# Four neighbouring rows of a down-projection chunk in one partition, with gate and up columns read with a step of four

## The chip, the cores and the metric

The kernel runs on one core of one Trainium2 chip. The metric is the device time of one execution in microseconds (us), the median of several executions. The engines are TensorE (PE; its loads of the stationary operand are shown as PEld), VectorE (DVE), ScalarE (ACT), GpSimd (POOL) and SyncE (SP), which issues nearly all DMAs; 16 DMA engines move the data.

## What is computed

Two layers of an encoder for 256 rows (tokens) of 1024 features in float32. Each layer has a mixer (three kinds of attention between two projections) and a mixture of experts. The change touches only the experts. Cut to them, the reference is:

```python
# per token: one of 4 groups, then 2 of its 8 experts; 32 experts per layer
def expert_block(args):
    xb, e = args
    h = jax.nn.silu(xb @ w_gate[e]) * (xb @ w_up[e])   # (rows, 1024) @ (1024, 512), twice
    return h @ w_down[e]                               # (rows, 512) @ (512, 1024)
```

The result of each token's two experts is multiplied by its gates and added to x. The weights w_gate and w_up are (2, 32, 1024, 512) and w_down is (2, 32, 512, 1024), all float32, so each expert has three matrices of 2 MiB.

## The kernel before

**Weights.** A ring of eight slots of 16 KB per partition (`ring`, lines 181 and 46 to 47) takes every large weight as a chunk of 2 MiB, one DMA each, issued by SP in a fixed order (lines 366 to 393): six chunks of the input projection, two of the output projection, and then per expert gate, up and down. A chunk goes into slot c % 8. Before each issue SP waits for the slot's semaphore `slot_free` (line 389); PE raises it when it is through with the chunk (lines 1419, 1420 and 1441). Each slot has a semaphore `slot_full` that the DMA raises on landing and that PE waits for (line 1397). Since the eight slots are in use one after the other, the DMAs run ahead of PE by up to eight chunks. All experts are computed for every layer, whichever tokens chose them, for at most 32 tokens each; a loop for experts with more tokens follows (line 1462) and does nothing with these inputs.

**Layouts.** The views at lines 309 and 310 put rows 8p to 8p+7 of gate and up into partition p, which are 8 x 512 neighbouring numbers of the tensor, 16 KB. The view at line 311 puts rows p, 128+p, 256+p and 384+p of down into partition p, four pieces of 1024 numbers (4 KB). The chunk views at lines 313 to 318 only name the 4096 numbers of a partition as (8, 512) or (4, 1024).

**The work per expert on PE** (lines 1444 to 1455; `ROUNDS` is 4 rounds of `BODY` = 8 experts, each with two groups of four). `tokens` gathers the tokens of four experts at once into `xg` by matmuls with a 0/1 matrix (line 1353). `products` waits for gate and up and runs `gate_up` (line 1364): for each of the eight row blocks j, four matmuls of 32 stationary columns (the tokens) and 256 moving columns (weights). The four go to four column groups of the array (tile_position 0, 32, 64, 96): gate's first and second half, up's first and second half. They write 4 x 32 partitions of `gu_ps`. The trace has two matmul records for each float32 matmul, so 64 per expert. ACT copies `gu_ps` to `h_rows` (line 616, recorded at its helper's line 466). `turned` releases the gate and up slots and transposes `h_rows` in two blocks of 128 columns (line 1372), after which partition d of block c holds column 128c + d of each half; it also transposes the gates (line 1374). ACT and DVE form silu(gate) x up in `hid` (lines 595, 963 to 971). `down` (line 1380) runs, for k = 0 to 3, a matmul of `hid[:, b, k % 2, k // 2]` with `down_chunk(s)[:, k]`: block k % 2 and half k // 2 of `hid` must be the expert features that row k of the down chunk holds in each partition. ACT copies the result to `y`, and `scatter` (line 1388) multiplies it by the transposed gates and adds it into four banks for all 256 tokens.

The order in the steady state is written out by hand: products(e), down_of(e-1), turned(e), add(e-1). PE is in order, so a wait for a chunk in `products` holds all behind it.

Other lines that the prediction speaks of: line 680 and line 877 (DVE, the normalised rows; both write with a step of 128 numbers, except line 680 in its last use), line 871 (DVE, an addition of 512 contiguous numbers), line 1333 (PE, bf16 matmuls of zeros that keep it busy while the router's result is awaited), and line 369 (the chunks of the input projection, whose pieces are 512 numbers of a row, 2 KB).

Of the kernel before, what the change touches and what calls it, by code (L numbers as in the profile page):

```python
# [44 lines left out]
KE = D_EXPERT // P  # L45
SLOTS = 8
SLOT = KD * 512
CAP = 32
QUAD = P // CAP
HALF = D_EXPERT // 2  # L50
# [105 lines left out]
def trunk(nc, x_d, w_in, w_out, norm_mix, norm_ffn, rel_bias, lam_q1, lam_k1, lam_q2, lam_k2,  # L156
# [4 lines left out]
    with ctx:  # L161
# [13 lines left out]
        gu_ps = pv[:, 0, 0:HALF]  # L175
# [38 lines left out]
        def take(n):  # L214
            taken[0] += n
            assert taken[0] <= arena.shape[1]
            return arena[:, taken[0] - n:taken[0]]
# [24 lines left out]
        xg = take(2 * KD * P).rearrange("p (b j s) -> p b j s", b=2, j=KD)  # L242
# [65 lines left out]
        wout_v = w_out.rearrange("l (k p) n -> l p k n", k=KD)  # L308
        gate_v = w_gate.rearrange("l e (p j) d -> (l e) p j d", j=KD)
        up_v = w_up.rearrange("l e (p j) d -> (l e) p j d", j=KD)  # L310
        down_v = w_down.rearrange("l e (k p) n -> (l e) p k n", k=KE)

        def chunk(s, n):

            return ring[:, s, 0:KD * n].rearrange("p (j n) -> p j n", j=KD)
# [4 lines left out]
        def nk(t):  # L320
            return P * (t + 1)
# [735 lines left out]
        def _(pe):  # L1057

            mm, turn_ = nc.tensor.matmul, nc.tensor.transpose
# [8 lines left out]
            with pe.Fori(0, DEPTH) as l:  # L1068
# [34 lines left out]
                def z_rows(out, i, n, c, m, t):  # L1103

                    for j in range(KD):
                        ins = mm(out, xT[:, j, t * P:(t + 1) * P], chunk(i, n)[:, j, c:c + m],  # L1106
                                 start=(j == 0), stop=(j == KD - 1))
                    return ins
# [83 lines left out]
                for t in range(TOK):  # L1192
                    ins = z_rows(bank[:, 256 * t:256 * t + 256], 1, 512, 0, 256, t)
# [3 lines left out]
                for t in range(TOK):  # L1197
                    pe.wait_ge(cn_ready, at(l, 2, t + 1))
                    bank = tr_bank()
                    for k in range(3):  # L1200
                        ins = turn_(bank[:, k * P:(k + 1) * P], cn[:, t, k * P:(k + 1) * P], ident)
# [5 lines left out]
                for t in range(TOK):  # L1207
                    for k in range(2):
                        ins = mm(pv[:, 0, 192 * t:192 * t + 192], cT[:, k, t * P:(t + 1) * P], wuq[:, k, :],
                                 start=(k == 0), stop=(k == 1))  # L1210
# [8 lines left out]
                for u in range(0, 8, 2):  # L1219
                    t = u // 4  # L1220
                    banks = tr_bank(), tr_bank()
                    for m in range(2):
                        for i in range(2):
                            a = IDX_DIM * (u % 4 + i)
                            ins = mm(banks[i][:, m * nk(t):(m + 1) * nk(t)], zT[a:a + 32, 12 + m, t * P:(t + 1) * P],
                                     zT[a:a + 32, 14, 0:nk(t)], start=True, stop=True, tile_position=(a, 0))
# [5 lines left out]
                for pad in (qpad, kpad):  # L1232
                    bank = tr_bank()
                    for g in range(2):
                        for t in range(TOK):
                            ins = turn_(bank[:, g * SEQ + t * P:g * SEQ + (t + 1) * P],
                                        pad[:, t, 2 * g:2 * g + 2, :].rearrange("p h d -> p (h d)"), ident)
# [120 lines left out]

                def gate_up(sg, su, q, c):

                    halves = [chunk(s, 512)[:, :, h:h + HALF] for s in (sg, su) for h in (0, HALF)]
                    for j in range(KD):
                        for i, w in enumerate(halves):
                            ins = mm(gu_ps[i * CAP:(i + 1) * CAP, :], xg[:, q, j, c:c + CAP], w[:, j, :],  # L1364
                                     start=(j == 0), stop=(j == KD - 1), tile_position=(0, i * CAP),
                                     skip_group_check=True)
                    return ins
# [24 lines left out]
                with pe.Fori(0, ROUNDS) as m:  # L1392
# [13 lines left out]
                    def products(e):  # L1406

                        q, i, c = e // QUAD, e % QUAD, 3 * e
                        if i == 0:
                            pe.wait_ge(wide_read, at(r, WIDE, gather_use(q) + 1))  # L1410
                        landed(c)
                        landed(c + 1)
                        gate_up(c % SLOTS, (c + 1) % SLOTS, q, i * CAP).then_inc(gu_done, 1)
# [48 lines left out]
                with pe.If(more > 0):  # L1462
                    with pe.Fori(0, more) as k:
                        i = done + k
                        pe.wait_ge(o_pick, i + 1)
                        gather(0, CAP)[1].then_inc(o_wide, 1)
                        pe.wait_ge(o_wide_read, i * 2 + 1)
                        pe.wait_ge(over_full[0], i * 16 + 16)
                        pe.wait_ge(over_full[1], i * 16 + 16)
                        gate_up(0, 1, 0, 0).then_inc(o_gu, 1)  # L1470
                        pe.wait_ge(o_gu_read, i + 1)
                        turns(0, 0).then_inc(o_h, 1)
                        pe.wait_ge(o_hid, i + 1)
                        pe.wait_ge(over_full[2], i * 16 + 16)
                        down(2, 0, 0)
                        down(2, 0, 1).then_inc(o_wide, 1)
                        pe.wait_ge(o_wide, i * 2 + 2)
                        pe.sem_inc(over_free, 1)
                        pe.wait_ge(o_wide_read, i * 2 + 2)
                        pe.wait_ge(o_pgt_read, i + 1)  # L1480
                        scatter(0, 0)
                        scatter(0, 1).then_inc(o_comb, 1)
                pe.nop()

                for t in range(TOK):
                    for half in range(2):
                        ins = mm(acc[t][half], zeros[:, 0:P], zeros[:, P:P + 512], start=False, stop=True,
                                 skip_group_check=True)
# [43 lines left out]
```

## Time and profile before

| | us |
|---|---|
| Median of 3 runs | 1404.72 (1402.9 to 1407.91) |
| Profiled execution, its own time | 1402.78 |
| Its span, first to last instruction | 1400.2 |
| PE busy | 1109.2 (79%) |
| PE weight loads busy | 626.7 (45%) |
| DVE busy | 346.1 (25%) |
| ACT busy | 236.6 (17%) |
| POOL busy | 19.6 (1%) |

The span is the time between the first and the last instruction on the engines; the time of the execution has 2.6 us more around it. Busy shares are means over stages of different kinds: in each layer the mixer runs first, with few loads, and then the expert rounds, with loads all the time. PE's clock is given as the granted share of 2.4 GHz, and its mean over the span is 0.887. A time that a DMA takes "to landing" runs from its issue on SP's queue until its data have all arrived, so it contains the time in which the chunks ahead of it are moved.

### The profile page before, as it was taken

Reading aid. Unit: us, or ns where it says so; the run is one execution under the profiler, and the core shown is the slowest. Engines: PE = TensorE matmul, PEld = TensorE weight load, DVE = VectorE, ACT = ScalarE, POOL = GpSimd, SP = SyncE. Lnnn points to the kernel's source line nnn. Section 1 sums busy time; section 2 is a strip of 40 time slices with the busy share of each in tenths; the row PEclk is TensorE's granted clock in tenths of the full one; section 3 lists DMA queues with packets and bytes.
Section 4 is the critical chain, followed back from the end, with each engine's and each line's share of the span. In section 5 each row is a group of like instructions: output and inputs, shape, how many; then the busy total and the mean of one; then the engine's idle time right before and its main releaser. Section 6 shows DMA issues by size and latency. Waiting matters only on the chain.

```text
span 1400.2 us, 19949 instructions
## 1 busy us (share of the span) xinstructions
PE 1109.2 (79%) x7926; PEld 626.7 (45%) x7930; DVE 346.1 (25%) x954; ACT 236.6 (17%) x578; POOL 19.6 (1%) x45
## 2 busy tenths in 40 slices
PE   7379888888796877878779887898778777778776
PEld 3357645443443433344337664454344334434432
DVE  2035445312111211211121363551121121112112
ACT  2013321111111111111121242111111111111111
POOL 1000000000000000000000000000000000000000
PEclk9779889998898989899889888999799889889988
DMA  7592314799999999999995113069999999999993
GB/s 236 98 396 95 121 61 155 287 420 419 420 424 416 421 422 419 421 422 418 416 378 198 61 61 121 9 257 419 423 418 419 422 421 419 420 423 417 421 423 144
DMA packets 80143, 446.72 MB, mean 319 GB/s; under 512 B 9864, under 2 KB 15272, under 8 KB 63656
## 3 DMA queue, kind: packets, MB, share of 16 engines
q1 hardware_dynamic: 75816, 442.73, 78.3%
q10 hardware_dynamic: 4224, 2.46, 0.6%
q8 instruction: 84, 1.38, 0.4%
q14 instruction: 19, 0.16, 0.0%
HBM read 442.55 MB, written 2.62 MB: 318 GB/s over the span
## 4 chain that ended last, share of the span: by engine, by line
PE 49%; DMA 35%; issue 9%; DVE 3%; ACT 3%; ACTq 1%; POOL 0%; DVEq 0%; PEldq 0%; SPq 0%; POOLq 0%
DMA ring<-in_w_up 34%; PE pv L1364 14%; PE pj L1100 7%; PE tr L1380 5%; PE pj L1281 4%; PE pj L1106 3%; PE tr L1353 3%; PE pj L1388 3%; PE lg L1388 2%; ACT arena L466 2%; PE lg L1135 1%; PE pv L1166 1%; ACTq L350 1%; PE tr L1148 1%; PE pv L1301 1%
## 5 line engine op out<-in xcount | busy, mean ns | idle before, releaser
L1364 PE MATMUL pv<-ring,arena 128*32 128x256 f32 x4096 | 307.3, 464 | 162.6 <-DMA ring<-in_w_up 147.3
L1364 PEld LDWEIGHTS pv<-ring,arena 128*32 128x32 f32 x4096 | 165.3, 133 | 311.1 <-issue 211.7
L966 DVE TENSOR_SCALAR arena<-arena 128x128 f32<-128x128 f32 x64 | 14.5, 227 | 739.9 <-ACT arena L596 739.9
L466 ACT ACTIVATE arena<-tr 128x512 f32<-128x512 f32 (+3 forms) x200 | 111.2, 564 | 279.3 <-PE tr L1353 129.5
L1388 PE MATMUL pj<-arena 128*128 128x512 f32 x256 | 131.7, 596 | 0.0
L1388 PE MATMUL lg<-arena 128*128 128x512 f32 x256 | 130.7, 592 | 0.0
L466 ACT ACTIVATE arena<-pv 128x256 f32<-128x256 f32 x64 | 24.5, 383 | 581.7 <-PE pv L1364 581.7
L1380 PE MATMUL tr<-ring,arena 128*32 128x512 f32 x1024 | 122.1, 593 | 0.0
L1100 PE MATMUL pj<-xT,ring 128*128 128x256 f32 (+1 forms) x480 | 115.7, 402 | 3.7 <-ACT arena L466 2.7
L1100 PEld LDWEIGHTS pj<-xT,ring 128*128 128x128 f32 (+1 forms) x480 | 93.5, 198 | 24.3 <-issue 5.9
L1353 PE MATMUL tr<-arena,rows 128*128 128x128 f32 x512 | 71.5, 307 | 24.5 <-issue 23.4
L1353 PEld LDWEIGHTS tr<-arena,rows 128*128 128x128 f32 x512 | 70.0, 222 | 34.3 <-issue 32.2
L1388 PEld LDWEIGHTS lg<-arena 128*128 128x128 f32 x256 | 48.6, 190 | 61.2 <-issue 61.2
L1281 PE MATMUL pj<-ring,xT 128*128 128x512 f32 x128 | 63.2, 646 | 5.6 <-ACT xT L466 5.6
L1106 PE MATMUL pj<-ring,xT 128*128 128x408 f32 (+2 forms) x192 | 65.1, 496 | 0.4 <-ACT xT L466 0.4
L967 DVE RECIPROCAL arena<-arena 128x128 f32<-128x128 f32 x64 | 61.0, 953 | 2.2
L1388 PEld LDWEIGHTS pj<-arena 128*128 128x128 f32 x256 | 43.6, 190 | 37.3 <-issue 30.6
L1380 PEld LDWEIGHTS tr<-ring,arena 128*32 128x32 f32 x1024 | 33.7, 110 | 52.7 <-issue 43.7
L1106 PEld LDWEIGHTS pj<-ring,xT 128*128 128x128 f32 x192 | 36.0, 190 | 26.0 <-issue 23.2
L466 ACT ACTIVATE arena<-pj 64x256 f32<-64x256 f32 (+3 forms) x56 | 24.1, 433 | 129.7 <-PE pj L1100 91.6
L1281 PEld LDWEIGHTS pj<-ring,xT 128*128 128x128 f32 x128 | 25.5, 207 | 35.2 <-issue 28.5
L1372 PEld LDWEIGHTS pv<-con,arena 128*128 128x128 f32 x128 | 12.8, 140 | 56.5 <-issue 56.5
(170 smaller groups left out, 683.8 us busy)
## 6 DMA issues: line engine op xcount, KB each, us to landing
ring<-in_w_gate SPq DMA_DIRECT2D x64, 2048.0 KB, 30.7
ring<-in_w_up SPq DMA_DIRECT2D x64, 2048.0 KB, 22.0
ring<-in_w_down SPq DMA_DIRECT2D x64, 2048.0 KB, 26.6
ring<-in_w_in SPq DMA_DIRECT2D x10, 2048.0 KB, 19.7
ring<-in_w_out SPq DMA_DIRECT2D x4, 2048.0 KB, 20.0
ring<-in_w_in SPq DMA_DIRECT2D x2, 1760.0 KB, 19.5
bias_lines<-ring SPq DMA_DIRECT2D x1, 1536.0 KB
x<-in_x SPq DMA_DIRECT2D x1, 1024.0 KB, 5.0
```

The costliest lines, as they stand in the source:

```text
L350: eng.dma_start(dst, src).then_inc(small_in, 16)
L466: return nc.scalar.activation(out, in_, ACT.Copy, **k)
L966: own.link(v.tensor_scalar(sig, e_neg[:, b], 1.0, None, ALU.add))
L967: own.link(v.reciprocal(sig, sig))
L1100: ins = mm(out, w[:, j], xT[:, j, :], start=(j == 0), stop=(j == KD - 1))
L1106: ins = mm(out, xT[:, j, t * P:(t + 1) * P], chunk(i, n)[:, j, c:c + m], start=(j == 0), stop=(j == KD - 1))
L1135: ins = mm(lg[:, u % 2, m * n:(m + 1) * n], q[a:a + d, t * P:(t + 1) * P], k[a:a + d, 0:n], start=True, stop=True)
L1281: ins = mm(pj[:, half], xT[:, k, t * P:(t + 1) * P], chunk(6 + half, 512)[:, k, :], start=(k == 0), stop=(k == KD - 1))
L1353: ins = mm(wide_ps[:, j * n:(j + 1) * n], rows[:, t, j * P:(j + 1) * P], pick[:, q, t, 0:n], start=(t == 0), stop=(t == TOK - 1))
L1364: ins = mm(gu_ps[i * CAP:(i + 1) * CAP, :], xg[:, q, j, c:c + CAP], w[:, j, :], start=(j == 0), stop=(j == KD - 1), tile_position=(0, i * ...
L1380: ins = mm(tr[k * CAP:(k + 1) * CAP, half], hid[:, b, k % 2, k // 2, :], down_chunk(s)[:, k, 512 * half:512 * half + 512], start=True, sto ...
L1388: ins = mm(acc[t][half], pgT[:, b, t, :], y[:, 512 * half:512 * half + 512], start=False, stop=False, skip_group_check=True)
```

## The change

The down chunk is loaded with rows 4p to 4p+3 in partition p, which are 16 KB in one piece of the tensor. Row k of partition d is then expert feature 4d + k instead of 128k + d. So that `hid` has the same features in its blocks, `gate_up` reads the columns of gate and up with a step of four: of the two halves of each, the first has features 4d and then 4d + 1 (d = 0 to 127), the second 4d + 2 and then 4d + 3. The number of matmuls, their shapes, and all that follows stay as they are.

```diff
-        down_v = w_down.rearrange("l e (k p) n -> (l e) p k n", k=KE)
+        down_v = w_down.rearrange("l e (p k) n -> (l e) p k n", k=KE)
...
                 def gate_up(sg, su, q, c):
 
-                    halves = [chunk(s, 512)[:, :, h:h + HALF] for s in (sg, su) for h in (0, HALF)]
+                    halves = [chunk(s, 512).rearrange("p j (d k) -> p j k d", k=KE)[:, :, h:h + KE // 2, :]
+                              for s in (sg, su) for h in (0, KE // 2)]
                     for j in range(KD):
                         for i, w in enumerate(halves):
-                            ins = mm(gu_ps[i * CAP:(i + 1) * CAP, :], xg[:, q, j, c:c + CAP], w[:, j, :],
+                            ins = mm(gu_ps[i * CAP:(i + 1) * CAP, :], xg[:, q, j, c:c + CAP], w[:, j],
                                      start=(j == 0), stop=(j == KD - 1), tile_position=(0, i * CAP),
                                      skip_group_check=True)
```

## Rows read from the trace of the kernel before

**Rows 1.** The page's head: span, busy times, DMA in 40 slices, packets by size.

```profile
span 1400.2 us, 19949 instructions
PE 1109.2 (79%) x7926; PEld 626.7 (45%) x7930; DVE 346.1 (25%) x954; ACT 236.6 (17%) x578; POOL 19.6 (1%) x45
...
DMA  7592314799999999999995113069999999999993
...
DMA packets 80143, 446.72 MB, mean 319 GB/s; under 512 B 9864, under 2 KB 15272, under 8 KB 63656
```

**Rows 2.** The chain that ended last, by line, with shares of the span.

```profile
DMA ring<-in_w_up 34%; PE pv L1364 14%; PE pj L1100 7%; PE tr L1380 5%; PE pj L1281 4%; PE pj L1106 3%; PE tr L1353 3%; PE pj L1388 3%; PE lg L1388 2%; ACT arena L466 2%; PE lg L1135 1%; PE pv L1166 1%; ACTq L350 1%; PE tr L1148 1%; PE pv L1301 1%
```

**Rows 3.** Two windows, one in each layer's expert rounds.

```profile
core 0: us, PE busy (x) PEld busy (x) DVE busy (x) ACT busy (x) POOL busy (x), PEclk, DMA share, GB/s
265.00:700.00 435.00, 344.44 (x2929) 177.43 (x2931) 71.69 (x165) 61.12 (x130) 0.00 (x0) 0.88 1.01 420
940.00:1375.00 435.00, 340.75 (x2916) 175.62 (x2918) 71.72 (x166) 61.12 (x130) 0.00 (x0) 0.88 1.01 418
```

**Rows 4.** Timeline of PE early in layer one's rounds: start, us, line, releaser.

```profile
266.46 3.66 PE L1364 MATMUL pv<-ring,arena 128*32 128x256 f32 x64
...
275.79 3.66 PE L1364 MATMUL pv<-ring,arena 128*32 128x256 f32 x64
...
285.02 3.73 PE L1353 MATMUL tr<-arena,rows 128*128 128x128 f32 x32
290.18 3.66 PE L1364 MATMUL pv<-ring,arena 128*32 128x256 f32 x64 [1.43 <-DMA ring<-in_w_up]
```

**Rows 5.** Timeline of PE, the same work some experts later.

```profile
319.96 6.40 PE L1364 MATMUL pv<-ring,arena 128*32 128x256 f32 x64 [3.89 <-DMA ring<-in_w_up]
...
334.90 5.35 PE L1364 MATMUL pv<-ring,arena 128*32 128x256 f32 x64 [2.81 <-DMA ring<-in_w_up]
```

**Rows 6.** A window in the first of these bursts; columns as in rows 3.

```profile
320.00:325.00 5.00, 5.00 (x48) 2.62 (x52) 0.00 (x0) 0.00 (x0) 0.00 (x0) 0.50 1.06 432
```

**Rows 7.** Four issues in a row, and each one's time to landing.

```profile
296.33 0.33 SPq L393 DMA_DIRECT2D ring<-in_w_up  x1
DMA to landing us min/median/max: 23.5/23.5/23.5
...
296.76 0.38 SPq L391 DMA_DIRECT2D ring<-in_w_down  x1
DMA to landing us min/median/max: 28.2/28.2/28.2
...
297.33 6.67 SPq L393 DMA_DIRECT2D ring<-in_w_gate  x1
DMA to landing us min/median/max: 32.5/32.5/32.5
...
312.84 0.33 SPq L393 DMA_DIRECT2D ring<-in_w_up  x1
DMA to landing us min/median/max: 21.9/21.9/21.9
```

**Rows 8.** Two windows with input projection chunks in flight; columns as in rows 3.

```profile
705.00:710.00 5.00, 5.00 (x25) 1.61 (x23) 2.10 (x5) 0.63 (x2) 0.00 (x0) 1.00 1.05 386
710.00:715.00 5.00, 4.45 (x12) 1.76 (x12) 0.90 (x2) 0.60 (x1) 0.00 (x0) 1.00 1.05 383
```

**Rows 9.** Timeline of PE: bf16 matmuls of zeros at full clock.

```profile
920.84 1.46 PE L1333 MATMUL pj<-zeros 128*128 128x512 bf16 x6
```

**Rows 10.** Groups of DVE by form: a stepped and a contiguous write.

```profile
L877 DVE TENSOR_TENSOR rows<-x,gain_ffn 128x512 f32<-128x512 f32 x8 | 8.0, 1047 | 0.1
...
L871 DVE TENSOR_TENSOR x<-pj,x 128x512 f32<-128x512 f32 x8 | 5.5, 692 | 2.0 <-PE pj L1281 1.3 <-DVE ssq L834 0.4
```

**Rows 11.** Timeline: the first burst of layer one, and the first refill.

```profile
250.55 5.27 PE L1364 MATMUL pv<-ring,arena 128*32 128x256 f32 x64 [4.69 <-ACT arena L466]
...
256.39 0.38 SPq L391 DMA_DIRECT2D ring<-in_w_down  x1
```

**Rows 12.** Timeline of PE: layer two's first burst and last scatter.

```profile
927.22 3.66 PE L1364 MATMUL pv<-ring,arena 128*32 128x256 f32 x64 [0.94 <-ACT arena L466]
...
1388.72 1.02 PE L1388 MATMUL lg<-arena 128*128 128x512 f32 x2
```

## The prediction

> **What bounds the kernel now.** I began with the page's head [rows 1]. The span is 1400.2 us, TensorE (PE) is busy for 79% of it, VectorE 25%, ScalarE 17%. A busy PE is not yet the bound, so the next rows matter more: the DMA line shows nines in two long stretches, slices 9 to 20 and 27 to 39, at about 420 GB/s, and DVE and ACT are at 1 or 2 tenths there. These stretches are the expert rounds of the two layers. The chain that ended last [rows 2] puts 34% of the span on a weight load, by far its largest entry. Over 435 us of each layer's rounds [rows 3] the DMA engines are fully occupied (share 1.01) and move 420 and 418 GB/s, PE is busy 344 and 341 us.
>
> An expert costs the DMA three chunks of 2 MiB (gate, up, down), 3 x 2.097 MB / 419 GB/s = 15.0 us. PE alone is faster. Early in a layer, when eight prefetched slots leave it a backlog, its gate/up bursts start 9.33 us apart (266.46, 275.79) [rows 4], of which a burst of 64 matmuls takes 3.66 us. A gather for four experts adds 290.18 - 285.02 less the 1.43 us of waiting for a load, 3.7 us, or 0.9 per expert. So PE needs 10.3 us per expert against 15.0 and waits for the loads from then on: 3.89 and 2.81 us before the bursts at 319.96 and 334.90 [rows 5]. In those bursts it is also slow, because it has idled: the granted clock is 0.50 (1.2 GHz) at 320 to 325 us [rows 6] and the burst takes 6.40 us. Conclusion: **what ends last in the rounds is the stream of weights**, and an edit that makes a chunk land sooner is worth its full amount, as long as PE stays under the chunk time.
>
> **Part 1: the down chunk's layout.** Before, a partition takes rows p, 128+p, 256+p, 384+p: four runs of 4 KB, 512 packets per chunk. Gate and up already take 16 KB in a run per partition. The packet line bears this out [rows 1]: of 80143 packets 63656 are under 8 KB, so 16487 are larger, which is the 128 gate and up chunks x 128 partitions = 16384. After, a partition takes rows 4p to 4p+3, one run of 16 KB; 64 x 384 = 24576 packets go. Does a run of 16 KB land sooner? The issues and the times to landing of four chunks in a row give it [rows 7]: up 296.33 + 23.5 = 319.8, down 296.76 + 28.2 = 325.0, gate 297.33 + 32.5 = 329.8, up 312.84 + 21.9 = 334.7. The gaps are 5.2 for down, 4.8 and 4.9 for the others. I formed the same gap for 29 chunks of each kind in the first layer, from the down chunk issued at 263.71 to the one issued at 675.24: median 5.1 for down, 4.9 for gate and for up. A second estimate is the mean: 15.0 us per expert by the bandwidth against 3 x 4.9 = 14.7, though a few gaps of 5.4 to 6.4 us are in that mean which need not be the layout's. A third is from the other side, the layout with 2 KB runs that w_in has: 383 to 386 GB/s [rows 8], 2.097 MB / 384 = 5.46 us per chunk. Per engine a chunk is 8, 32 or 64 packets, so a packet costs (5.1 - 4.9) / 24 = 8 ns by the first pair and (5.46 - 5.1) / 32 = 11 ns by the second. The same kind of cost at both steps is why I take it to be the packets and not the order of the chunks.
>
> The saving is 0.2 us per down chunk, with bounds of 0.15 (gaps rounded the other way) and 0.28 (the mean). It counts where PE waits for the stream: 29 gaps per layer, 58 in all. The first chunks of a round are prefetched and hidden, and the last down chunk of a layer lands while PE is still in its last burst. **58 x 0.2 = 11.6 us saved**, 8.7 to 16 by the bounds.
>
> The Trainium skill, "DMA: Bandwidth & Descriptors", section "Why small descriptors are slow", gives a packet about three extra cycles against one for every 32 bytes. By that, 131 x 4 cycles become 515, an estimate of 1.7% of a down chunk, and the sum would be 5 us instead of 11.6. The measured gaps decide here.
>
> **Part 2: SyncE.** The number of issues and waits is unchanged. A gate issue that follows a down issue holds SP for 6.67 us [rows 7], others take 0.33; with a quarter of the packets queued I expect this to shrink. Worth nothing: each chunk is queued over 20 us before it lands, so the stream has no hole to fill.
>
> **Part 3: the step of four in the gate/up matmuls.** Instructions, shapes, loads of the stationary side and order stay; h_rows column c x 128 + d now is expert feature 4d + k, which is what the new down rows need, so nothing else moves. What changes is how PE reads its moving operand: neighbouring columns are 16 bytes apart instead of 4. No row shows PE doing that. From below: nothing. PE takes an fp32 column in 3.66 us / (16 x 256) = 0.89 ns, while in the warm-up matmuls (bf16, 512 columns) it takes one in 1.46 / (6 x 512) = 0.48 ns [rows 9], so fp32 leaves its port half of the time per element. A gain is excluded, since no column is dropped and the arithmetic sets 0.89. From above: VectorE writing with a step of 512 bytes takes 1047 ns for 512 elements, 2.04 ns each, against 692 ns for a contiguous one of the same size [rows 10]. At 2.04 ns a burst takes 16 x 256 x 2.04 = 8.4 us, 4.7 more. A further end: a burst is four column groups that read at the same time; if a step of 16 bytes made them take turns, it would be 4 x 3.66 = 14.6 us. I take the lower end, by PE's own row, which is nearer than another engine's write. What covers it: the slack of 14.7 - 10.3 = 4.4 us per expert, so a burst may grow by a factor of up to 2.2 before it sets the time. Even covered it costs at the two ends of each layer: the first refill waits for the first burst (SP issues the down chunk at 256.39, after the burst that began at 250.55) [rows 11], and the last burst stands behind the last up chunk.
>
> The Trainium skill, "SBUF — State Buffer", on the 16-byte cachelines, speaks against the change: a line wants at least two hits for full bandwidth, and here every element is the first of its own line. It gives no price; no run so far shows PE in that case.
>
> **The sum.** 1402.78 us was the profiled execution (span 1400.2 and 2.6 around it); minus 11.6 is 1391.2. It lies 1.9 under the median of the runs shown, 1404.72, and that median is what I forecast against: **1393 us**, 0.8% less.
>
> **Rivals.** (A) The forecast: strided reads free or hidden. A factor of 1.5 would still cost 1.8 us at each layer's start and about 1 at its end, 6 in all: 1399, faster too. Chance 0.55.
> (B) The factor is about 2. Period 10.3 + 3.7 = 14.0, still under 14.7, but 3.7 later at the start and some 2 at the end of each layer, + 11.4 against - 11.6: 1404. For it: VectorE's stepped write takes 1.5 times its contiguous one [rows 10], a factor of this size. Chance 0.10.
> (C) **PE becomes the bound**, at line 1364, from a factor of 2.2 up. At 2.04 ns per element the period is 10.3 + 4.7 = 15.0 us; a layer's rounds are then 32 x 15.0 = 480 us instead of 462 (927.2 to 1389.7, the first burst to the last scatter) [rows 12], +18 per layer, +36: about 1440. At a factor of 2.5 the period is 15.8 and the time near 1490, at 4 it is 21.3 and the time about 1840. For it: four groups want lines from the same 32 KB at once. Against: the half-idle port of [rows 9]. Chance 0.29. By the skill's cacheline rule this is the case to come, if its penalty is more than a factor of two.
> (D) The change doesn't do what it says for the time: the 16 KB runs are cut up again, or the down chunk is slower for another reason. Then 1405. Gate and up, with the same kind of run, speak against it. Chance 0.06.
>
> **The numbers.** A measurement of this kernel can tell about 0.3%, 4.2 us, from no change. Faster by more: 0.55 (A). Within: 0.16 (B, D). Slower by more: 0.29 (C). The range reaches from 1387 (0.28 us per chunk) to 1470, which holds A, B, D and C up to a factor of about 2.4; left out are some 0.15 above and 0.03 below. A's own range is 1387 to 1399.
>
> **What would show it.** Right: packets about 55,600 instead of 80143; landing gaps of 4.9 for down; GB/s near 428 in the rounds; bursts of 64 at 3.66 us at full clock and PE's distances of 9.33 early in a layer unchanged; waits for the up chunk somewhat shorter. Wrong: L1364's mean well above 464 ns with bursts over 8 us at full clock, PE in the chain where the load was, and GB/s below 410 (C); bursts near 7.3 us and the time unmoved (B); down gaps still 5.1 (D).

## The result, and the profile after

The changed kernel takes 1421.22 us (median of 4 runs, 1416.72 to 1430.97) against 1403.81 us (4 runs). The ratio is 1.0131, with a 95% interval of 1.0102 to 1.016: **slower by 1.3%**, where 0.8% faster was forecast. The profiled execution took 1430.97 us with a span of 1429.0; it is the slowest of the four, and the differences of traces below are to be read with that in mind.

First the page's head, and the chain by line, which answer to [rows 1, 2]:

```profile
span 1429.0 us, 19953 instructions
PE 1279.7 (90%) x7930; PEld 617.7 (43%) x7930; DVE 346.1 (24%) x954; ACT 236.8 (17%) x578; POOL 19.6 (1%) x45
...
DMA packets 55559, 446.57 MB, mean 313 GB/s; under 512 B 9865, under 2 KB 15273, under 8 KB 30889
...
PE pv L1365 33%; PE pj L1389 8%; PE tr L1381 8%; PE lg L1389 8%; PE pj L1100 7%; PE tr L1353 5%; PE pj L1281 4%; PE pj L1106 3%; PE pv L1373 2%; ACT arena L466 1%; PE pv L1375 1%; PE lg L1135 1%; PE pv L1166 1%; ACTq L350 1%; PE tr L1148 1%
```

The packets fell as counted (55559; the forecast had 55,600). The load that held 34% of the chain is gone from it, and the gate/up matmuls (L1365, which was L1364) have its place. PE is busy for 170 us more. The windows over the expert rounds, as in [rows 3], say the same: PE is busy 413 and 416 of 435 us, at almost full clock, and the DMA engines move less than before, 414 and 403 GB/s against 420 and 418.

```profile
265.00:700.00 435.00, 413.09 (x2884) 172.70 (x2880) 71.06 (x163) 61.16 (x130) 0.00 (x0) 0.98 0.99 414
940.00:1375.00 435.00, 416.09 (x2942) 172.56 (x2944) 79.39 (x191) 61.19 (x130) 0.00 (x0) 0.99 0.96 403
```

PE's timeline at the start of the first layer's rounds, and over the change from the first round to the second:

```profile
251.20 7.50 PE L1365 MATMUL pv<-ring,arena 128*32 128x256 f32 x64 [5.32 <-ACT arena L466]
...
273.09 7.43 PE L1365 MATMUL pv<-ring,arena 128*32 128x256 f32 x64
...
286.20 7.44 PE L1365 MATMUL pv<-ring,arena 128*32 128x256 f32 x64
...
360.59 1.02 PE L1389 MATMUL lg<-arena 128*128 128x512 f32 x2
365.30 5.46 PE L1353 MATMUL tr<-arena,rows 128*128 128x128 f32 x32 [3.69 <-issue]
371.69 7.66 PE L1365 MATMUL pv<-ring,arena 128*32 128x256 f32 x64 [0.93 <-ACT arena L466]
```

A burst of 64 takes 7.44 us where it took 3.66 [rows 4], and no burst waits for a load any more [compare rows 5]. Bursts are 286.20 - 273.09 = 13.11 us apart instead of 9.33. The change of rounds, which the prediction did not count, is the second thing to see: 3.69 us of idle time that PE's row puts down to no wait ("issue"), then a gather of 5.46 instead of 3.73 us. The kernel before has the same at its change of rounds:

```profile
355.08 5.46 PE L1353 MATMUL tr<-arena,rows 128*128 128x128 f32 x32 [3.61 <-issue]
```

### The profile page after: what moved, and what is told of

Same layout as the page of the kernel before. It is cut to its first block, busy times and chain, and to the rows that moved or that the text cites. A ratio compares the mean times of both kernels' runs of the same rounds, so it can differ in the third digit from the quotient of the medians.

```text
span 1429.0 us, 19953 instructions
## 1 busy us (share of the span) xinstructions
PE 1279.7 (90%) x7930; PEld 617.7 (43%) x7930; DVE 346.1 (24%) x954; ACT 236.8 (17%) x578; POOL 19.6 (1%) x45
## 2 busy tenths in 40 slices
DMA packets 55559, 446.57 MB, mean 313 GB/s; under 512 B 9865, under 2 KB 15273, under 8 KB 30889
## 3 DMA queue, kind: packets, MB, share of 16 engines
q8 instruction: 75, 1.23, 0.4%
## 4 chain that ended last, share of the span: by engine, by line
PE 84%; issue 9%; DVE 3%; ACT 2%; ACTq 1%; DMA 0%; POOL 0%; DVEq 0%; SPq 0%; POOLq 0%
PE pv L1365 33%; PE pj L1389 8%; PE tr L1381 8%; PE lg L1389 8%; PE pj L1100 7%; PE tr L1353 5%; PE pj L1281 4%; PE pj L1106 3%; PE pv L1373 2%; ACT arena L466 1%; PE pv L1375 1%; PE lg L1135 1%; PE pv L1166 1%; ACTq L350 1%; PE tr L1148 1%
## 5 line engine op out<-in xcount | busy, mean ns | idle before, releaser
L1365 PE MATMUL pv<-ring,arena 128*32 128x256 f32 x4096 | 477.2, 632 | 17.3 <-ACT arena L466 17.3
L1365 PEld LDWEIGHTS pv<-ring,arena 128*32 128x32 f32 x4096 | 154.5, 126 | 313.7 <-issue 295.3
## 6 DMA issues: line engine op xcount, KB each, us to landing
ring<-in_w_out SPq DMA_DIRECT2D x4, 2048.0 KB, 20.6
```

## The experiments

Several kernels below leave features unmatched, as their expectations say. In most of these the second layer's router sees other values, one expert gets more than 32 tokens, and the loop for such experts runs once (65 chunks of each kind are loaded, not 64). Their whole times are thus too long by an amount that has nothing to do with the question. The first layer is free of this, so I compare **the first layer's rounds**, from the start of the first burst to the first matmul behind the rounds. In the kernel before that is 713.69 - 250.55 = 463.1 us, after the change 731.92 - 251.20 = 480.7. This measure has a flaw: it contains PE's idle time behind the last scatter, which is 0 in some traces and up to 3.9 us in others. The column beside it ends at the start of the last scatter row (712.61 - 250.55 = 462.1 before, 727.38 - 251.20 = 476.2 after) and leaves that out. Both are of one profiled execution of each kernel. The ratios are to runs of the kernel before that were made beside each kernel, whose medians lie between 1403.22 and 1404.35.

| kernel | burst, us | first layer's rounds, us | to the last scatter, us | median, us | ratio to before (95%) |
|---|---|---|---|---|---|
| before | 3.66 | 463.1 | 462.1 | 1403.81 | |
| the change | 7.44 | 480.7 | 476.2 | 1421.22 | 1.0131 (1.0102 to 1.016) |
| the change again | 7.44 | 481.6 | 476.7 | 1425.43 | 1.014 (1.0101 to 1.0179) |
| layout alone | 3.66 | 457.3 | 455.5 | 1411.51 (one expert more) | 1.0054 (1.0033 to 1.0075) |
| step alone | 7.44 | 478.2 | 473.7 | 1446.12 (one expert more) | 1.029 (1.0257 to 1.0323) |
| pairs | 3.84 | 458.1 | 457.2 | 1392.65 | 0.9905 (0.9877 to 0.9932) |
| step of two | 3.85 | 465.7 | 461.0 | 1399.82 | 0.9966 (0.9943 to 0.9989) |
| only gate's groups stepped | 7.57 | 481.9 | 477.3 | 1450.71 (one expert more) | 1.0312 (1.0275 to 1.0349) |
| step in the scatter | 3.66 | 467.3 | 465.5 | 1438.45 (one run, one expert more) | |
| step of eight | 7.57 | 478.0 | 477.1 | 1462.55 (one run, one expert more) | |
| half stepped | 5.55 | 460.6 | 456.1 | 1398.91 (one run) | |
| the change, rounds filled | 7.44 | 479.4 | 474.8 | 1438.47 | 1.0237 (1.02 to 1.0274) |

### The layout alone

```diff
-        down_v = w_down.rearrange("l e (k p) n -> (l e) p k n", k=KE)
+        down_v = w_down.rearrange("l e (p k) n -> (l e) p k n", k=KE)
```

> Only the down chunk's layout is changed; gate and up are read contiguously as before, so the hidden features meet other rows of the down chunk than in the reference. Theory 1 (the prediction's part 1 holds, the loss is PE's alone): bursts of 64 stay at 3.66 us, down's landing gap falls from 5.1 to 4.9 us, and the time falls by 58 x 0.2 = 11.6 us to about 1392. Theory 2 (the gaps belong to the order of the chunks, and the layout gives nothing): within 2 us of 1404. Theory 3 (the layout itself slows PE or the stream): above 1410.

The whole time, 1411.51, seems to fit theory 3, and would have misled without the trace, whose issues count 65 chunks of each kind. The first layer has the answer: its rounds take 706.80 - 249.46 = 457.3 us, 5.8 less than before, with bursts of 3.66. In the window over them the DMA moves 426 GB/s instead of 420:

```profile
265.00:700.00 435.00, 346.42 (x2985) 179.25 (x2984) 73.05 (x168) 62.97 (x134) 0.00 (x0) 0.89 1.01 426
```

Down chunks land 4.92 us after up (median of 28 gaps), where it was 5.1. Twice 5.8 us would be the forecast's 11.6, though the second layer can't be compared here. Theory 1 stands; theory 3 falls, and so does theory 2.

### The step alone

```diff
-        down_v = w_down.rearrange("l e (p k) n -> (l e) p k n", k=KE)
+        down_v = w_down.rearrange("l e (k p) n -> (l e) p k n", k=KE)
```

(against the changed kernel)

> Only the step of four in the gate and up reads; the down chunk keeps its four runs of 4 KB, so the hidden features meet other rows of the down chunk than in the reference. Theory 1 (the stepped read doubles the burst and PE becomes the bound): bursts at 7.44 us, PE busy for 95% of the rounds, and the same time as with the whole change, 1417 to 1424, since the stream is no longer the bound. Theory 2 (both parts of the change cost something, or help each other): more than 5 us away from the whole change's 1421.

Its first layer's rounds take 727.49 - 249.30 = 478.2 us, 2.5 less than the whole change's, with the same burst of 7.44. The median of 1446.12 misses the expected 1417 to 1424, since the expectation left the extra expert out. The 2.5 us are not the layout's: the three changes of rounds have 13.2 us of idle time and gathers of 16.4 us in all here, against 14.2 and 17.9 in the change. So the step by itself makes the whole loss, and the layout's gain doesn't show once PE is the bound.

### One read for two neighbours

The same down layout, with the same features in the same column group, but in the order 4d, 4d + 1 and then the next d. Each 16 bytes are visited once, for two columns. The transposes then sort the features.

```diff
-                    halves = [chunk(s, 512).rearrange("p j (d k) -> p j k d", k=KE)[:, :, h:h + KE // 2, :]
+                    halves = [chunk(s, 512).rearrange("p j (d k) -> p j d k", k=KE)[:, :, :, h:h + KE // 2]
...
-                        turn_(h_ps[:, c].rearrange("p h s -> p (h s)"), h_rows[:, c * P:(c + 1) * P], ident)
+                        turn_(h_ps[:, c].rearrange("p h s -> p (h s)"), h_rows.rearrange("p (d k) -> p k d", k=2)[:, c], ident)
```

> The down layout of the change, but each column group reads two neighbouring numbers and then steps over two (step 16 bytes, pairs), and the transposes read h_rows with a step of two (8 bytes) to sort the features. Theory 1 (a column costs extra only when it is alone on its 16 bytes): bursts back at 3.66 us, transposes unchanged, time about 1392. Theory 2 (any read that is not contiguous, or whose pattern has two free dimensions, runs at half speed): bursts at 7.4 us, time about 1421. Theory 3 (cost goes with the number of 16-byte lines per burst, 8192 numbers in 4096 lines now): bursts about halfway, 5.5 us, hidden under the loads, time 1392 to 1400.

PE's timeline of this kernel, the issues and landings of an up and a down chunk, and the window over the rounds:

```profile
269.60 3.83 PE L1365 MATMUL pv<-ring,arena 128*32 128x256 f32 x64
...
279.17 3.84 PE L1365 MATMUL pv<-ring,arena 128*32 128x256 f32 x64
```

```profile
285.50 0.33 SPq L393 DMA_DIRECT2D ring<-in_w_up  x1
DMA to landing us min/median/max: 21.8/21.8/21.8
...
285.93 0.38 SPq L391 DMA_DIRECT2D ring<-in_w_down  x1
DMA to landing us min/median/max: 26.2/26.2/26.2
286.50 0.33 SPq L393 DMA_DIRECT2D ring<-in_w_gate  x1
```

```profile
265.00:700.00 435.00, 355.66 (x2988) 183.06 (x2984) 73.06 (x168) 63.85 (x135) 0.00 (x0) 0.89 1.01 426
```

The burst is at 3.84 us, 5% above the contiguous one, and the distance 9.57. Down lands at 285.93 + 26.2 = 312.1, 4.8 us after up (307.3); over 29 such gaps the median is 4.9, as it is for gate and up, where it was 5.1 before [rows 7]. The gate issue behind it takes 0.33 us and not 6.67. Theory 1 holds up to those 5%, and the kernel takes **1392.65 us, 0.95% less than before** (interval 0.68 to 1.23%). It leaves nothing of the computation out and beats both kernels. The transposes pay a little for their step of two: their matmul records go from 299 to 332 ns and their weight loads from 140 to 206 ns, hidden under the loads.

### Only gate's groups stepped

```diff
-                    halves = [chunk(s, 512).rearrange("p j (d k) -> p j k d", k=KE)[:, :, h:h + KE // 2, :]
-                              for s in (sg, su) for h in (0, KE // 2)]
+                    stepped = chunk(sg, 512).rearrange("p j (d k) -> p j k d", k=KE)
+                    plain = chunk(su, 512).rearrange("p j (k d) -> p j k d", k=KE)
+                    halves = [w[:, :, h:h + KE // 2, :] for w in (stepped, plain) for h in (0, KE // 2)]
```

> The whole change, but only the two column groups that read gate have the step of four; the two that read up are contiguous, so up's features no longer meet gate's. Theory 1 (each column group is slowed by itself, at 1.8 ns per column): the four run side by side and the burst still takes 7.4 us. Theory 2 (the four groups share what the read port can fetch, and the step makes them compete): two groups need less, the burst is near 5.5 us, and the time is at or below 1404.

```profile
250.66 7.57 PE L1366 MATMUL pv<-ring,arena 128*32 128x256 f32 x64 [5.03 <-ACT arena L466]
...
L1366 PE MATMUL pv<-ring,arena x4160: 379/626/673, 250.7 to 1436.8; 128*32 128x256 f32 x199
```

(The second line has the shortest, median and longest record of all 4160.) The burst takes 7.57 us with only two of the four groups stepped, so the groups don't share one reading capacity: theory 2 falls. Each stepped stream is slow by itself. The shortest records are 379 ns, the median of the kernel before, so I take it that the contiguous streams are not slowed but wait their turn behind the stepped ones in PE's order; the trace doesn't show that wait by itself.

### A step in the scatter matmuls

```diff
-                        ins = mm(acc[t][half], pgT[:, b, t, :], y[:, 512 * half:512 * half + 512],
+                        ins = mm(acc[t][half], pgT[:, b, t, :],
+                                 y[:, 512 * half:512 * half + 512].rearrange("p (d k) -> p k d", k=KE),
```

> The kernel before; only the scatter matmuls (one group over the full array) read y with a step of four, so their columns come out in another order. Theory 1 (the cost is each operand stream's own, 1.8 ns per column): a record that starts every 0.43 us takes 0.9 us or so, 512 x 1.8 ns. Theory 2 (it takes four column groups that read at once): the records stay 0.43 us apart. In the first layer the rounds then take 463 us plus what 8 x 0.5 = 4 us per expert add over the slack (theory 1), or 463 (theory 2).

PE's timeline: scatter, then the next burst.

```profile
262.15 1.96 PE L1388 MATMUL pj<-arena 128*128 128x512 f32 x2
263.93 1.98 PE L1388 MATMUL lg<-arena 128*128 128x512 f32 x2
...
269.44 3.66 PE L1364 MATMUL pv<-ring,arena 128*32 128x256 f32 x64
```

Two records take 263.93 - 262.15 = 1.78 us, 0.89 each or 1.74 ns per column, where they took 0.43. So one stream over the whole array is slowed by a factor of 2.07, about as much as the burst of four (7.44 / 16 / 256 = 1.82 ns, a factor of 2.03): theory 1. The first layer's rounds take 717.19 - 249.85 = 467.3 us. PE has about as much more work here as with the change, and yet the rounds are 13 us shorter. The trace differs at the changes of rounds: here the three have no idle time, none and 0.24 us, and the gathers run at full clock, where the change idles 3.69, 5.51 and 5.02 us. In the second and the third the longer scatter, which stands last in a round, may cover that time, as the filler does further down; the first seems to have nothing to cover (the count of packets there). The first of the three:

```profile
359.63 1.98 PE L1388 MATMUL lg<-arena 128*128 128x512 f32 x2
361.43 3.75 PE L1353 MATMUL tr<-arena,rows 128*128 128x128 f32 x32
```

### The size of the step

Two, with a down chunk of two runs of 8 KB per partition:

```diff
-        down_v = w_down.rearrange("l e (p k) n -> (l e) p k n", k=KE)
+        down_v = w_down.rearrange("l e (a p k) n -> (l e) p a k n", a=2, k=2)
...
-                    halves = [chunk(s, 512).rearrange("p j (d k) -> p j k d", k=KE)[:, :, h:h + KE // 2, :]
-                              for s in (sg, su) for h in (0, KE // 2)]
+                    halves = [chunk(s, 512)[:, :, h:h + HALF].rearrange("p j (d k) -> p j k d", k=2)
+                              for s in (sg, su) for h in (0, HALF)]
```

> The down chunk holds two runs of 8 KB per partition (rows 2p, 2p+1 and 256+2p, 256+2p+1), and each column group reads its contiguous half with a step of two (8 bytes), so two columns of a stretch of 16 bytes are used, though not side by side with a third in between. The transposes are as before. Theory 1 (what costs is a column alone on its 16 bytes): bursts near 3.7 to 3.9 us; 256 packets per chunk instead of 512, at 8 ns per packet and engine 16 x 8 = 0.13 us per down chunk, so 58 x 0.13 = 7.5 us saved, 1396. Theory 2 (any step above one costs half the speed, and the pairs were fast because each second number is a neighbour): bursts at 7.4 us, time about 1421.

Eight, over the whole row block:

```diff
-                    halves = [chunk(s, 512).rearrange("p j (d k) -> p j k d", k=KE)[:, :, h:h + KE // 2, :]
-                              for s in (sg, su) for h in (0, KE // 2)]
+                    halves = [chunk(s, 512).rearrange("p j (d k) -> p j k d", k=8)[:, :, h:h + 4, :]
+                              for s in (sg, su) for h in (0, 4)]
```

> The whole change, but the columns are read with a step of eight (32 bytes) over all 512 of a row block, so the features come out in another order than the down chunk's. Theory 1 (a column pays once for being alone on its 16 bytes): bursts at 7.44 us as with a step of four. Theory 2 (the cost grows with the distance): bursts above 8 us, towards 14.

The bursts, of the kernel with a step of two and of that with a step of eight:

```profile
257.59 3.85 PE L1365 MATMUL pv<-ring,arena 128*32 128x256 f32 x64
```

```profile
259.57 7.57 PE L1365 MATMUL pv<-ring,arena 128*32 128x256 f32 x64
```

Steps of 1, 2, 4 and 8 numbers give 3.66, 3.85, 7.44 and 7.57 us. The cost is a jump between 8 and 16 bytes and then nearly nothing: theory 1 in both. The step of two takes the time down to 1399.82, ratio 0.9966, less than the 7.5 us expected. Its down chunks land 4.95 us after up (median of 28), between 5.1 and 4.9 as the packet count (63750 in all) would have it. But up to the last scatter the first layer's rounds take 461.0 us, only 1.0 less than before, and three gate chunks landed 6.0 to 6.9 us after down. I have no cause for those. So this run doesn't confirm a fixed price per packet.

### Half of the row blocks stepped

```diff
+                    plain = [chunk(s, 512)[:, :, h:h + HALF].rearrange("p j (k d) -> p j k d", k=2)
+                             for s in (sg, su) for h in (0, HALF)]
...
-                        for i, w in enumerate(halves):
+                        for i, w in enumerate(stepped if j % 2 else plain):
```

(`stepped` is the change's `halves`)

> The whole change, but four of the eight row blocks are read contiguously, so their features don't match the others'. It sets the burst between the two. Theory 1 (the whole change lost because a burst of 7.44 us exceeds what the loads cover, and the slack per round of eight is 119.6 - 92.8 = 26.8 us, 3.35 per expert): bursts near 5.5 us, 1.9 more per expert are covered, and the first layer's rounds take about 457 + 3 = 460 us, against 481 with the whole change and 463 before. Theory 2 (a slower burst always costs its own amount): 457 + 32 x 1.9 = 518 us.

```profile
259.03 5.55 PE L1367 MATMUL pv<-ring,arena 128*32 128x256 f32 x64
...
711.99 1.04 PE L1490 MATMUL pj<-zeros 128*128 128x512 bf16 x2 [3.50 <-issue]
```

The rounds take 711.99 - 251.41 = 460.6 us for an expected 460. That they meet so closely is in part luck, since 3.5 us of it is the idle time behind the last scatter, which the kernel before doesn't have. Up to the last scatter they take 456.1 us, about half a us more than with the layout alone: 1.9 us more per burst is covered, 3.8 is not. A slower burst costs nothing up to the slack and its excess after that.

### The change of rounds

To ask what the idle time of 3.5 to 5.5 us at a round's start is, I ran the change once more as a measure, and beside it the change with matmuls of zeros behind a round:

```diff
                     down_of(BODY - 1)
                     add(BODY - 1)
+                    keep_warm(16)
```

> The whole change once more, as the measure for the kernel beside it: 1417 to 1424 us, first layer's rounds near 480 us.

> The whole change, and 16 bf16 matmuls of zeros (0.22 us each at full clock, 3.5 us) at the end of each round of eight experts. They add nothing to the result. Theory 1 (the idle time of 3.5 to 5.5 us ahead of a round's first gather is a delay of the jump back that runs on while queued matmuls are worked off, and the gather is slow only since PE has idled): the idle time all but vanishes, the gather takes 3.7 us instead of 5.5, a round costs 122.8 - 5.4 + 3.5 = 121 us, and the first layer's rounds take 480 - 3 x 2 + 3.5 = 478 us. Theory 2 (the delay starts only when the last matmul is done): 3.5 us more in each round, 480 + 14 = 494 us, and the time rises by 28 us.

The change again takes 1425.43 us (9 runs, without the slowest 1413.24 to 1434.17), filled 1438.47 (4 runs). A change of rounds in each, the plain one first:

```profile
365.47 5.46 PE L1353 MATMUL tr<-arena,rows 128*128 128x128 f32 x32 [4.98 <-issue]
...
1177.48 3.73 PE L1353 MATMUL tr<-arena,rows 128*128 128x128 f32 x32
```

```profile
361.25 3.40 PE L1333 MATMUL pj<-zeros 128*128 128x512 bf16 x15
366.52 3.83 PE L1353 MATMUL tr<-arena,rows 128*128 128x128 f32 x32 [1.87 <-issue]
```

Within the first layer theory 1 is borne out in part: the idle time shrinks from 4.98 to 1.87 us by about what the filler takes. The gather is back at 3.83 in two of the three changes; in the third it takes 5.46 after an idle time of 1.86. The rounds take 730.07 - 250.70 = 479.4, 2.2 less. But the whole got 13 us slower, which neither theory has. In the second layer the plain kernel has one change of rounds with no idle time at all (the row at 1177.48), and its round takes 1177.48 - 1060.48 = 117.0 us; the filled one idles each time. So the delay comes and goes, and the filler pays its 3.4 us in every round.

The traces show what goes with it. Beside the weights' queue the profile has one that it calls "instruction". In the 18 us around each of the plain kernel's five changes of rounds with idle time (14 before the gather's start, 4 behind it) this queue moves three packets; around the one at 1177.48 it moves none. Over the whole execution it moves 84 packets where all six changes have the delay, 75 where one is without and 66 where two are. From the pages of the kernel before, the change again and half stepped (no idle time at 472.59 and 1028.23):

```profile
q8 instruction: 84, 1.38, 0.4%
```

```profile
q8 instruction: 75, 1.23, 0.4%
```

```profile
q8 instruction: 66, 1.08, 0.3%
```

All twelve traces keep to this count if the scatter's kernel is read by its packets, which are missing at 361.43 alone. So the idle time goes with a transfer on the instruction queue, which I read as code fetched behind the jump back. Why some rounds do without it stays open. The kernel before has the delay six times too, while its loads go on at 420 GB/s, and the changed kernel's runs spread over 21 us even without the slowest, those of the kernel before over 8.

## Why the prediction was wrong

**Part 1, the layout: right** in the gap and in size. Forecast were gaps of 4.9 us and 11.6 us in all. The layout alone has gaps of 4.92 and shortened the first layer's rounds by 5.8 us, and the pairs kernel, which keeps the gain, took 1392.65 us for a forecast of 1393. That the gain is a price per packet is not shown: with half of the packets saved the first layer's rounds were 1.0 us shorter up to the last scatter, where all of them gave 6.5. The estimate from the Trainium skill, "DMA: Bandwidth & Descriptors", section "Why small descriptors are slow", was 5 us; the layout's measured gain is about 11, so three cycles per packet don't account for it.

**Part 2, SyncE:** the gate issue went from 6.67 to 0.33 us, as expected. No run tests its effect on the time by itself.

**Part 3, the step: this is what failed**, in two of its numbers. The first is the choice of the lower end, "nothing". I had argued that fp32 takes a column every 0.89 ns and bf16 one every 0.48 ns [rows 9], so that the port has time to spare for each fp32 number. The bf16 row was contiguous, and said nothing of how long a read takes that brings one useful number. That is 1.8 ns per column, whether the step is 16 or 32 bytes, in one stream or four. It is nearly the same at a lower clock: over the first part of the burst at 251.20 the mean granted clock was 0.64, and the burst took 7.50 us for 7.44.

```profile
251.00:255.00 4.00, 3.80 (x36) 1.77 (x40) 0.00 (x0) 0.00 (x0) 0.00 (x0) 0.64 0.03 6
```

VectorE's stepped write, 2.04 ns per element [rows 10], the row I put aside as further away, was the better one: it gave a burst of 8.4 us, and 7.44 was measured. That it came near is luck as far as the runs show, since it is another engine's write with a step of 512 bytes. The far end of 14.6 us, groups taking turns, was wrong too.

The Trainium skill, "SBUF — State Buffer", on the 16-byte cachelines, had the rule: two hits on a line for full bandwidth. The runs agree with it: two numbers per 16 bytes, side by side or with one between them, cost 5%, one number doubles the burst. I cited it and then gave it no weight because it had no price.

The second number is the slack. I took PE's time per expert as 9.33 + 0.9 = 10.3 us and the slack as 4.4 us, a factor of 2.2. With a measured factor of 2.03 the whole burst should still have been covered, case B. Two things were left out.

One is the change of rounds, once in eight experts, which stood in the trace of before as well (the row at 355.08). A round of the changed kernel takes 122.6 us (gathers at 365.30 and 487.85), of which 8 x 3.78 are the step; without it PE needs 92.3, where 8 x 10.3 = 82.4 was assumed. With the layout alone two rounds take 119.5 and 119.1 us (gathers at 353.72, 473.18 and 592.28). So the slack is 27 us per round, 3.4 per expert, and the burst needs 3.8.

The other is the first round of a layer, eight of whose 24 chunks have landed before it. From the first burst to the next round's gather the layout alone takes 353.72 - 249.46 = 104.3 us and the change 365.30 - 251.20 = 114.1, or 83.9 without the step. There the slack is 20.4 us, 2.6 per expert.

Beside the layout alone, the four rounds of the first layer (the last one up to its last scatter) cost the change 9.8, 3.1, 3.7 and 4.1 us, 20.6 in all; less the layout's 6.5 that is the 14.1 by which it is slower than before. Nearly half of the loss stands in the first round. This is a breakdown of measured rounds and no test; the test is the half-stepped kernel, whose 1.9 us more per burst lie under both slacks and were covered. In the second layer, where one change of rounds has no idle time, the rounds took 468.8 us up to the last scatter against 461.5, only 7.3 more. Of the 28.8 us by which the profiled execution's span is longer, another 5.6 lie between the first layer's last scatter and the second's first burst, of which 3.52 are idle time at the loop's end.

**The rivals.** What came is C's mechanism, PE as the bound at the line named, at the burst of B. C's price, 1440 for 2.04 ns per element, had two errors of opposite sign: a factor of 2.3 for 2.03, and a point of decision of 2.2 where a slack of 3.4 us makes it 1.9, less in the first round. The time of 1421 lies inside the stated range, on the side that I had given 0.29. D is excluded by the packets and the gaps.

## What to carry to other kernels

A change of layout that saves DMA packets can be paid for on the engine that reads the data: look at how many numbers of each 16 bytes its access takes, and take two neighbours at a time where the order allows it, which here turned 1.3% slower into 1% faster. When an engine hides behind another, work its slack out over the whole repeating unit, with the start of the loop in it, and not from the distance between two bursts in the middle; look at the first unit by itself, where prefetched loads have used up part of the slack. A kernel variant whose values steer a later branch has to be compared ahead of that branch.

## What the runs showed of the hardware

- TensorE reads an fp32 moving operand at 0.89 ns per column with a step of 1 number (0.84 for one stream over the full array), 0.94 with a step of 2 or in pairs, and 1.8 with a step of 4 or 8. The slowed rate holds for one stream over the full array (1.74 ns) and for each of four column groups alike.
- A stationary operand with a step of two numbers loads in 206 ns instead of 140 (128 columns, fp32; from the pairs kernel):

```profile
L1373 PEld LDWEIGHTS pv<-con,arena x128: 193/206/220, 259.3 to 1373.1; 128*128 128x128 f32 x128
```

- A chunk of 2 MiB lands 4.9 us after the one ahead of it in runs of 16 KB and 5.1 us in runs of 4 KB.
- PE's first matmul behind a jump back to the loop's start came up to 5.7 us after the last one ahead of it, less where matmuls were still queued (1.87 us behind 3.40 us of filler), and in some rounds at once. Where it came at once with nothing added in front, the instruction queue had moved no packet.
